# Per-stage RMS norm sums of a decoder step: GpSimd adds six chunks of squares, TensorE sums three operands instead of eight

## What is computed

```python
def rmsnorm(x, w, eps=NORM_EPS):
    xf = x.astype(jnp.float32)
    y = xf * lax.rsqrt(jnp.mean(xf * xf, axis=-1, keepdims=True) + eps)
    return (y * w.astype(jnp.float32)).astype(x.dtype)

def macaron_half(x, g, w_gate, w_up, w_down):
    h = rmsnorm(x, g)
    return x + 0.5 * ((jax.nn.silu(h @ w_gate) * (h @ w_up)) @ w_down)

# reference(), per layer i (...)
        xp = macaron_half(xp, *fa)
        up = rmsnorm(xp, norm_w[i, 1])
# mixer of the layer on up (...)
        xp = xp + mp
        xp = macaron_half(xp, *fb)
# after the last layer
    y_prompt = rmsnorm(xp, final_norm_w)
```

## Time and profile before

| | us |
|---|---|
| median of 3 runs | 3212.28 (3211.17 to 3214.03) |
| the profiled execution's own time | 3219.08 |
| its span, first to last instruction | 3216.4 |
| TensorE matmuls busy in the span | 3070.2 (95%) |
| VectorE busy | 1532.2 (48%) |
| ScalarE busy | 1066.7 (33%) |
| GpSimd busy | 163.8 (5%) |
| mean granted TensorE clock | 0.955 of full |

### The profile page before, as it was taken

One profiled execution on the slowest core, in us unless ns is written; L12 is line 12 of the kernel. 1 busy time (PEld: TensorE's weight loads), 2 busy tenths in 40 slices (PEclk: granted clock), 3 DMA queues, 4 the chain that ended last, 5 costly groups with the idle time before them and its releaser, 6 DMA issues.

```text
span 3216.4 us, 63024 instructions
## 1 busy us (share of the span) xinstructions
PE 3070.2 (95%) x28286; PEld 2761.8 (86%) x28286; DVE 1532.2 (48%) x2422; ACT 1066.7 (33%) x1595; POOL 163.8 (5%) x266
## 2 busy tenths in 40 slices
PE   7998999999999899999999899999999999999998
PEld 6995788799999776699999767789999957887997
DVE  4644343355565204365565453446556435443554
ACT  3432232244443213244443232224344322322432
POOL 1000002100000101000000000400000000021000
PEclk9999999899999997899999899899999989997999
DMA  6442401253554634254643432155454513012532
GB/s 220 152 152 84 141 29 33 53 183 125 189 162 133 214 131 156 65 164 134 192 150 125 161 106 84 43 155 160 153 172 142 172 69 115 29 33 53 173 126 69
DMA packets 333441, 402.32 MB, mean 125 GB/s; under 512 B 14746, under 2 KB 287295, under 8 KB 332813
## 3 DMA queue, kind: packets, MB, share of 16 engines
q1 hardware_dynamic: 320176, 353.20, 33.9%
q0 software_dynamic: 13072, 46.30, 4.9%
HBM read 384.90 MB, written 14.57 MB: 124 GB/s over the span
## 4 chain that ended last, share of the span: by engine, by line
PE 92%; DVE 4%; ACT 2%; issue 1%; DMA 0%; POOL 0%; DVEq 0%; ACTq 0%; POOLq 0%
PE bank L799 18%; PE bank L801 17%; PE bank L800 17%; PE bank L832 10%; PE bank L1381 4%; PE bank L1070 2%; PE bank L908 2%; PE bank L794 2%; PE bank L868 1%; PE bank L884 1%; PE bank L1049 1%; PE bank L1023 1%; PE bank L1154 1%; PE bank L1112 1%; ACT work L1853 1%
## 5 line engine op out<-in xcount | busy, mean ns | idle before, releaser
L799 PE MATMUL bank<-h_hi,w_hi 128*128 128x288 f32 x2816 | 837.2, 297 | 5.8 <-DVE h_lo L2164 5.5
L800 PE MATMUL bank<-h_hi,w_lo 128*128 128x288 f32 x2816 | 831.5, 295 | 0.0
L801 PE MATMUL bank<-h_lo,w_hi 128*128 128x288 f32 x2816 | 828.6, 294 | 0.0
L2172 DVE TENSOR_TENSOR w_lo<-ring,w_hi 128x2048 fp32r<-128x2048 f32 (+1 forms) x304 | 611.0, 2011 | 424.3 <-ACT w_hi L1791 424.3
L1791 ACT CAST w_hi<-ring 128x2048 fp32r<-128x2048 f32 (+1 forms) x304 | 511.1, 1683 | 636.9 <-PE bank L801 568.6
L799 PEld LDWEIGHTS bank<-h_hi,w_hi 128*128 128x128 f32 x2816 | 528.3, 188 | 7.9 <-DVE w_lo L2172 6.0
L801 PEld LDWEIGHTS bank<-h_lo,w_hi 128*128 128x128 f32 x2816 | 531.0, 189 | 0.0
L800 PEld LDWEIGHTS bank<-h_hi,w_lo 128*128 128x128 f32 x2816 | 529.3, 188 | 0.6
L799 PE MATMUL bank<-hid_hi,w_hi 128*128 128x288 f32 x1408 | 416.1, 296 | 0.0
L800 PE MATMUL bank<-hid_hi,w_lo 128*128 128x288 f32 x1408 | 415.4, 295 | 0.0
L801 PE MATMUL bank<-hid_lo,w_hi 128*128 128x288 f32 x1408 | 414.3, 294 | 0.0
(11 more groups left out here) (516 smaller groups left out, 3454.2 us busy)
## 6 DMA issues: line engine op xcount, KB each, us to landing
ring<-in_ffn_w_gate SPq DMA_DIRECT2D x88, 1024.0 KB, 5.4
ring<-in_ffn_w_up SPq DMA_DIRECT2D x88, 1024.0 KB, 7.9
ring<-in_ffn_w_down SPq DMA_DIRECT2D x64, 768.0 KB, 4.6
ring<-in_ffn_w_down SPq DMA_DIRECT2D x64, 640.0 KB, 5.8
ring<-in_rwkv_w_rkv SPq DMA_DIRECT2D x24, 1024.0 KB, 7.3
ring<-in_gdn_w_in SPq DMA_DIRECT2D x16, 1024.0 KB, 6.6
ring<-in_attn_w_qkv SPq DMA_DIRECT2D x12, 1024.0 KB, 6.3
ring<-in_rwkv_w_o SPq DMA_DIRECT2D x8, 1024.0 KB, 6.3
```

The costliest lines, as they stand in the source:

```text
L799: nc.tensor.matmul(out, w_hi_k, x_hi_k, start=start, stop=False)
L800: nc.tensor.matmul(out, w_lo_k, x_hi_k, start=False, stop=False)
L801: return nc.tensor.matmul(out, w_hi_k, x_lo_k, start=False, stop=stop)
L2172: nc.vector.tensor_tensor(w_lo[e][:, 0:k, :], raw, w_hi[e][:, 0:k, :], ALU.subtract).then_inc(w_lo_ready, 1)
```

## The change

ScalarE's squares of chunks 0 to 5 for a norm in front of a mixer, or of the final norm, move up into the down units of the feed-forward stage before, one behind each chunk's update; its `norm` is left with chunks 6 and 7. GpSimd, in a new `presum(k)`, adds squares 0 to 5 into `h[:, 5, :]` with five in-place additions in the order of the table `PRESUM`; each waits for the square of its first chunk, and two of them also for the additions before. It calls `presum` once at the start of the program and once at the end of each stage. TensorE waits for all five additions and then sums chunks 5, 6 and 7 with three calls instead of eight.

```diff
+        presummed = sem("presummed")
+        PRESUM = ((1, 0), (3, 2), (3, 1), (5, 4), (5, 3))
...
             def norm(k, at=0):
-                for c in range(CH):
+                pe.wait_ge(presummed, len(PRESUM) * (k + 1))
+                for c in (5, 6, 7):
                     pe.wait_ge(squared, 8 * k + c + 1)
-                    last = nc.tensor.matmul(bank[at][:, 0:NT], ones[:, :], h[:, c, :], start=(c == 0), stop=(c == CH - 1))
+                    last = nc.tensor.matmul(bank[at][:, 0:NT], ones[:, :], h[:, c, :], start=(c == 5), stop=(c == 7))
                 last.then_inc(ssq_done, 1)
...
         @block.scalar
         def _(act):
+            def square_x(k, c):
+                act.wait_ge(x_updated, 8 * k + c + 1)
+                nc.scalar.activation(h[:, c, :], x[:, c, :], ACT.Square).then_inc(squared, 1)
+
             def norm(k):
-                for c in range(CH):
-                    act.wait_ge(x_updated, 8 * k + c + 1)
-                    nc.scalar.activation(h[:, c, :], x[:, c, :], ACT.Square).then_inc(squared, 1)
+                for c in (6, 7):
+                    square_x(k, c)
                 root(k, 0)
...
                                 high_part(b + u + 1, e)
-                                if c < CH - 1 and v % 2 and leads_to_ffn(s):
-                                    gained(s + 1, c)
+                                if c < CH - 1 and v % 2:
+                                    if leads_to_ffn(s):
+                                        gained(s + 1, c)
+                                    else:
+                                        square_x(s + 1, c)
...
         @block.gpsimd
...
+            def presum(k):
+
+                for i, (c, other) in enumerate(PRESUM):
+                    pool.wait_ge(squared, 8 * k + c + 1)
+                    if other % 2:
+                        pool.wait_ge(presummed, len(PRESUM) * k + i)
+                    nc.gpsimd.tensor_tensor(h[:, c, :], h[:, c, :], h[:, other, :], ALU.add).then_inc(presummed, 1)
+                pool.wait_ge(presummed, len(PRESUM) * (k + 1))
...
+            presum(0)
             for s, (kind, n) in enumerate(stages):
...
                 if kind == "rwkv":
                     rwkv_loads(s, n)
                     rwkv(s, n)
+                presum(s + 1)
```

## The result

| | median, us | lowest to highest | runs |
|---|---|---|---|
| before, measured beside it | 3211.73 | 3202.75 to 3214.03 | 4 |
| after | 3178.47 | 3169.52 to 3180.54 | 4 |

The ratio is 0.9897 [0.9882, 0.9913]: 33.3 us faster, where 24.3 us were forecast. The profiled execution after took 3178.68 us (span 3177.0, mean granted clock 0.961; before 3216.4 and 0.955).

The account below looks back on a forecast made before the run. TensorE, busy 95% of the span, was taken as the bound. 19.4 + 8.2 = 27.6 us, less 1.5 and 1.8, gave 24.3 us: 3212.28 - 24.3 = 3188.0 us, range 3182 to 3197.

Parts of the forecast that it names:

- Sum matmuls in feed-forward stages: Eight feed-forward norms: ten matmuls less save 2.43 us each, all on the path, 19.4 us together.
- The first rival: Feed-forward stages: something other than TensorE sets the first unit's end, only the mixers' 8.2 us remain, 3204; chance 0.05.
- Mixers and end: Four mixers' heads and the final norm: the root starts 1.65 us earlier, then the table load limits; 8.2 us together.
- Moved squares: Squares moved between casts of the down units: cost ScalarE nothing new and hold up no cast.
- Additions: Five GpSimd additions a norm, 0.71 us each: a price only through VectorE, 1.5 us behind gated DeltaNet, 1.8 at the start.
- The lock: VectorE instructions with two SBUF inputs and GpSimd instructions reading SBUF exclude each other; 1.5 us taken behind the gated DeltaNet.
- The slower rival: Every norm: all five additions land on TensorE's path, 46 us against 27.6 gained, 18 us slower, 3231; chance 0.03.
- Set-up instruction: Program start: GpSimd's one-time set-up moves in front of its first addition; 0 taken, 3 us as the other end.
- the granted clock: Mixers' heads: TensorE's clock already falls there, the longer pause changes only when; 0 taken, 3 us either way.
- the rival on the clock: Four mixers: the longer pause makes the low clock last longer, up to 10.6 us back, 3199; chance 0.04.

Follow-up runs that it names:

- squares_moved: The changed kernel with only the squares moved into the down units, eight chunks summed and no additions: 3212.01 us, 1.0003 against the kernel before.
- no_adds: The changed kernel without GpSimd's additions and TensorE's wait for them, still summing three chunks: 3179.14 us, 0.9889 against the kernel before.
- adds_and_eight: The changed kernel with the additions kept but TensorE summing all eight chunks behind them: 3210.34 us, 0.9994 against the kernel before.
- before_gap1: The kernel before with 0.97 us of extra unread matmuls in each of three feed-forward stages next before mixers: 3204.55 us, 0.9986.
- after_again: The changed kernel with no edit, measured again on another chip: 3174.61 us, 0.9882 against the kernel before.
- four distances of the table: Both kernels with 0, 2.9, 5.8 and 8.8 us of extra matmuls over three feed-forward stages; with 8.8 us, before 3211.21 us, after 3187.96.

## Why the prediction was right or wrong

*Sum matmuls in feed-forward stages, 2.43 us each.* Right to 0.25 us: behind a feed-forward stage the reciprocal waits for `w_lo` as forecast, and a pair of stages gave 4.06 us. The first rival (nothing to gain there, 3204) is excluded by the stretches of 213.03 against 215.20 us.

*Mixers and end, 1.65 us each.* Right: 1.64 us of idle time are gone and the table load is late next.

*Moved squares, nothing.* Right: squares_moved 1.0003.

*Additions.* The mechanism was right, and the places too. The duration was mis-sized (0.84 us for 0.71). The lock cost 1.54 us behind the gated DeltaNet (1.5 said) and about 2.0 at the start (1.8 said). In the down units it costs nothing, as said: no_adds has the same stretches there. The slower rival would need 3.5 us of lock in every norm; adds_and_eight puts all thirteen together at 4.5 us.

*Set-up instruction, 0.* Right.

The terms that engines' rows show add up to some 23 us with the starts of the two profiles, and to some 24 with the mean starts, against 24.3.

**The step that failed** is the granted clock: "I take 0. Bounds: 1 us either way in each mixer, of which half is lost, and a full extra fall at the end; 3 us either way in all." It looked only at the pauses that the change touches, the heads, and the rival on the clock looked there too, and only for a loss. Over all runs before had 266 us of half-clock time (96 runs) and after 244 (8 runs); 22 us x 0.35 is 8 us of time, most of the 9 that were missing. In the two profiles it lay behind the heads: from 20 us behind the reciprocal on, attention had 78.5 us of it before and 64.9 after, the second rwkv 61.4 and 34.1 (before_gap1 54.6 and 34.1), while in the first 20 us nothing fell by more than 3.4 us. The repeat, after_again, had 54.6 and 47.7 us behind the heads of these two, so the places are less certain than the sum. **What made the half-clock time fall stays open** between two causes: the distances between the mixers, since before_gap1 has such a fall without the change, and GpSimd's additions, since adds_and_eight has it with the distances of before and no_adds mostly lacks it. The additions lengthen two places by 1.5 to 2 us and may act as such a shift themselves. That wasn't tested. The bounds should have been some 8 to 10 us either way: fixed shifts of at most 2.9 us a place moved the half-clock time between 234 and 275 us, 41 us x 0.35 = 14 us from end to end.

What the change is worth apart from that: averaged over the four distances of the table (mean spans less the added work, 3203.9 for before and 3175.0 for after) it gains 28.9 us, with 7.6 us less half-clock time, worth 2.7. That leaves 26.2 us against 23 to 24 of terms. **Open** are these 2 to 3 us: four distances are few, and the runs with gaps come from other chips than those of after. Open is also why the clock stays low longer at some distances than at others.

None of the seventeen other kernels is clearly faster than the changed one.

## What to carry to other kernels

Work on TensorE that stands in an unbroken run of matmuls is worth its full issue time; work ahead of a point where everyone waits is worth only the distance to whatever is late next, here a table load. GpSimd can take such work if its operands are ready early, and what it costs is read where VectorE has no slack. Where a kernel pauses often and its granted clock falls, expect a change to shift the clock's falls in places that it doesn't touch: check the terms on the stretches that repeat to a few hundredths of a us, compare both kernels at several fixed shifts, and hold a range open by about 0.3% for it.

## What the runs showed that I had not expected

- A kernel with more work can be faster: before_gap1, 2.9 us added, 4.5 us gained (0.9986 [0.9974, 0.9997]), through the granted clock (half-clock time 264 to 248 us).
- GpSimd's additions alone, with every sum as long as before, went with 20 us less half-clock time (adds_and_eight, 254 against 273 us beside it).
- Keeping TensorE busy through a pause held the clock at full there (1.00 for 0.73) without any gain in total (3178.38 us).
- GpSimd's additions and VectorE's `h_lo` take turns so evenly that both are slowed: 8.50 us for five additions (0.79 us at best each), 5.67 for eight `h_lo` (3.52 alone).
